# Two recurrences of a hybrid layer on Trainium2: operands of all tokens at once, chunk matrices 64 wide and stacked, inverse beside scan

## What is computed

```
def chunked_gated_delta_rule(q, k, v, g, beta):      # chunks of 64 tokens, gc = cumsum(g) in a chunk
    decay = where(causal, exp(gc_i - gc_j), 0)
    a_mat = where(strict, (k * beta) @ k.T * decay, 0)
    t_inv = inverse(eye + a_mat)
    u = t_inv @ (v * beta);  w = t_inv @ (k * beta * exp(gc))
    attn = q @ k.T * decay
    def step(state, ...):
        v_new = u_n - w_n @ state
        o_n = q_n @ state + attn_n @ v_new
        state = state * exp(gl_n) + k_n.T @ v_new

def rwkv7_scan(r, w, k, v, kk, a):                    # token by token in the reference
    sa = S @ -kk_t
    S = S * w_t + sa * (kk_t * a_t) + v_t * k_t
    o_t = S @ r_t
```

## Time and profile before

| | us |
|---|---|
| median of 3 runs | 3264.71 (3245.12 to 3265.23) |
| the profiled execution's own time | 3262.91 |
| its span | 3260.7 |
| mixer preparation | 338.5 to 386.6 |
| recurrences | 386.8 to 806.1 |

### The profile page before, as it was taken

The page is one execution under the profiler, slowest core; times in us unless marked ns, Lnnn a source line. Parts: engine busy times, 40 slices in busy tenths (PEclk is TensorE's granted clock), DMA queues, the critical chain, the costliest instruction groups (busy, mean ns, idle before and its releaser), DMA issues. The chain is left out here.

```text
span 3260.7 us, 35943 instructions
## 1 busy us (share of the span) xinstructions
PE 2840.7 (87%) x13881; PEld 2265.9 (69%) x13881; DVE 1667.9 (51%) x3102; ACT 1060.9 (33%) x2178; POOL 19.2 (1%) x58
## 2 busy tenths in 40 slices
PE   6967287886899659979899899997997989989999
PEld 5865277775688547657677688885765767768887
DVE  4225555554766355675433566644567543344444
ACT  2215211111432245454422322224454452232221
POOL 0000100000000000000000000000000000000000
PEclk8987578776999879989999999998998999999999
DMA  3210000001666202101133355521210213322221
GB/s 131 92 17 8 14 1 1 1 1 28 201 195 197 85 27 78 52 1 60 49 84 99 116 170 192 187 84 52 78 52 1 82 27 84 99 78 104 103 78 52
DMA packets 212210, 249.42 MB, mean 76 GB/s; under 512 B 13295, under 2 KB 125898, under 8 KB 212042
## 3 DMA queue, kind: packets, MB, share of 16 engines
q1 hardware_dynamic: 177056, 193.30, 18.6%
q10 hardware_dynamic: 34986, 53.84, 5.0%
HBM read 243.70 MB, written 2.10 MB: 75 GB/s over the span
## 5 line engine op out<-in xcount | busy, mean ns | idle before, releaser
L1892 ACT ACTIVATE weights_hi<-weight_ring 128x512 fp32r<-128x512 f32 (+1 forms) x240 | 143.9, 602 | 433.9 <-PE bank L1933 408.5
L1909 DVE TENSOR_TENSOR weights_lo<-weight_ring,weights_hi 128x512 fp32r<-128x512 f32 (+1 forms) x240 | 156.4, 654 | 236.3 <-ACT weights_hi L1892 236.2
L1933 PE MATMUL bank<-h_hi,weights_hi 128*128 128x512 f32 x512 | 209.7, 410 | 16.6 <-DVE h_lo L1909 9.5
L2659 ACT ACTIVATE weights_hi<-weight_ring 128x1024 fp32r<-128x1024 f32 x128 | 135.3, 1057 | 265.5 <-PE bank L2739 264.7
L2739 PE MATMUL bank<-h_hi,weights_hi 128*128 128x512 f32 x512 | 204.3, 399 | 19.4 <-DVE h_lo L340 19.4
L2218 PE MATMUL bank<-chunk_hi,h_hi 128*128 128x512 f32 x448 | 184.7, 412 | 30.4 <-DVE h_lo L340 26.0
L2739 PE MATMUL bank<-h_lo,weights_hi 128*128 128x512 f32 x512 | 204.3, 399 | 0.0
L1933 PE MATMUL bank<-h_lo,weights_hi 128*128 128x512 f32 x512 | 204.1, 399 | 0.0
L1933 PE MATMUL bank<-h_hi,weights_lo 128*128 128x512 f32 x512 | 202.1, 395 | 0.0
L2739 PE MATMUL bank<-h_hi,weights_lo 128*128 128x512 f32 x512 | 201.8, 394 | 0.0
L2739 PE MATMUL bank<-hidden_hi,weights_hi 128*128 128x512 f32 x512 | 200.2, 391 | 0.0
(11 more groups left out here) (446 smaller groups left out, 5757.0 us busy)
## 6 DMA issues: line engine op xcount, KB each, us to landing
arena<-in_ada_w ACTq DMA_DIRECT2D x48, 1024.0 KB, 5.3
weight_ring<-in_w_in SPq DMA_DIRECT2D x21, 2048.0 KB, 7.8
weight_ring<-in_w_in SPq DMA_DIRECT2D x65, 512.0 KB, 5.3
weight_ring<-in_w_mlp_up SPq DMA_DIRECT2D x16, 2048.0 KB, 8.3
weight_ring<-in_w_mlp_down SPq DMA_DIRECT2D x16, 2048.0 KB, 8.1
weight_ring<-in_w_out SPq DMA_DIRECT2D x6, 2048.0 KB, 8.0
weight_ring<-in_w_in SPq DMA_DIRECT2D x10, 1024.0 KB, 6.6
weight_ring<-in_w_branch_a SPq DMA_DIRECT2D x16, 512.0 KB, 6.4
```

The costliest lines, as they stand in the source:

```text
L1892: act.activation(hi, src, ACT.Copy).then_inc(*hi_done.one())
L1909: dve.tensor_tensor(lo, src, hi.bitcast(F32), ALU.subtract).then_inc(*lo_done.one())
L1933: ins = pe.matmul(out, ws[a_][:, n % PIECES, k - k0, :], tile["x"][b_][:, k, :], start=k + a_ + b_ == 0, stop=last[n] and k == k1 - 1 and ...
L2659: act.activation(ws[0][:, t % 2], src[t // 4][:, :, c % 4 * P:c % 4 * P + P], ACT.Copy)\
```

## The change

It rewrites the recurrences in four respects.

1. `mixer_preparation`: `wa` moves into the weight ring. POOL makes more masks: `same`, and for `until`, `strict`, identity and the six levels a packed copy of 64 columns, in which rows 0 to 63 hold the block of chunk 0 and rows 64 to 127 that of chunk 1. DVE waits for the step "masks", and this step now comes right after POOL has zeroed two paddings, in front of all masks.
2. A new stage `operands` forms the operands of all 512 tokens at once, in tensors of 1024 columns (four tiles of 256), gdn first and then rwkv. PE turns and sums, ACT evacuates, takes exponentials and squares, DVE multiplies. The by-feature operands have a pair of heads above each other in the 128 rows.
3. `inverse(kind)`: the chunk matrices are 64 x 64, chunk 0's in rows 0 to 63 and chunk 1's in rows 64 to 127, four heads side by side: 256 columns instead of 512. A product is eight matmuls of 64 x 64 with 64 columns instead of four of 128 x 128 with 128. Each kind has two banks for it.
4. `scan(kind)` has two other banks. `side_by_side` runs five rounds: round i holds the inverses of tile i and the scans of tile i - 1, four generators in turn on each engine. Normalisation, gate and transposes of y are done for each tile within its round.

The diff, cut to its core:

```diff
-        self.bank = [nc.alloc_psum_tensor(f"bank{b}", [P, 512], F32) for b in range(8)]
+        self.banks = nc.alloc_psum_tensor("bank", [P, 8, 512], F32)
+        self.bank = [self.banks[:, b, :] for b in range(8)]
...
                 seq(pool.memset(rwT[:, :, 0:1], 0.0))
+                pool.memset(self.scratch[0:1, 1:2], 0.0).then_inc(*self.pool_ready.step("masks"))
...
-                for m, sign, base in ((self.until, 1, 0), (self.beyond, -1, -1), (self.strict, 1, -1)):
+                for m, sign, base in ((self.until, 1, 0), (self.beyond, -1, -1), (self.strict, 1, -1),
+                                      (self.same, 0, 0)):
...
+                for c in range(2):
+                    rows = slice(c * CH, (c + 1) * CH)
+                    for dst, full in ((self.until_p, self.until), (self.strict_p, self.strict),
+                                      (self.ident_p, self.ident)):
+                        pool.tensor_copy(dst[rows, :], full[rows, rows]).then_inc(*self.pool_order.one())
+                    pool.tensor_copy(self.levels_p[rows], levels[rows, :, rows]).then_inc(*self.pool_order.one())
+                pool.memset(self.scratch[0:1, 0:1], 0.0).then_inc(*self.pool_ready.step("zeros"))
...
-                dve.wait_ge(*self.pool_ready.after("zeros"))
+                dve.wait_ge(*self.pool_ready.after("masks"))
...
+    def operands(self):
...
+                def turn_in(srcT, first, c0, b0):
+                    for i in range(NT):
+                        for c in range(2):
+                            ins = pe.transpose(two(b0)[:, i * MIX + c * P:i * MIX + (c + 1) * P],
+                                               srcT[:, c0 + c, first + i * P:first + (i + 1) * P], self.ident[:])
...
+                did(tt(per_head(tm["kn"]), per_head(two(2)), over(ss[:, 1, :]), ALU.mult), "kn")
+                after("kn")
+                did(tt(per_head(tm["kb"]), per_head(tm["kn"]), over(beta), ALU.mult), "kb")
...
+    def inverse(self, kind, buffers, bank0):
...
+        order = [(s, c) for s in range(H) for c in range(2)]
...
+            def product(out, lhsT, rhs, other=None):
+                for s, c in order:
+                    o = out if other is None or c == 0 else other
+                    ins = pe.matmul(o[rows(c), s * CH:(s + 1) * CH], lhsT(s, c), rhs(s, c), start=True, stop=True)
...
+                product(bank[x], of(M), of(T1)).then_inc(*pe_done.step((i, "X", l)))
+                yield
+                pe.wait_ge(*act_done.after((i, "X", l)))
+                if l > 1:
+                    pe.wait_ge(*dve_done.after((i, "TT", l - 1)))
+                if l < LEVELS - 1:
+                    product(bank[d], of(TT), of(X)).then_inc(*pe_done.step((i, "dT", l)))
+                product(bank[x], of(X), of(TT)).then_inc(*pe_done.step((i, "dTT", l)))
+                yield
...
+    def scan(self, kind, buffers, bank0):
...
+                pe.matmul(last[rows(c), 4 * CH:], self.zeros[rows(1 - c), :],
+                          self.levels_p[rows(1 - c)].rearrange("p l u -> p (l u)")[:, 0:4 * CH], start=True, stop=False)
+                of_state(1 - c, i, c).then_inc(*pe_done.step((i, "RS", c)))
+                yield
+                pe.wait_ge(*pe_done.after((i, "RS", c)))
...
+            yield
+            yield
+            pe.wait_ge(*dve_done.after((i, "y")))
+            for c in range(2):
+                ins = pe.transpose(self.bank[bank0][:, c * P:(c + 1) * P], y[:, c * P:(c + 1) * P], self.ident[:])
...
         def side_by_side(which, engine):
-            running = [p[which](engine) for p in programs]
-            while running:
-                running = [g for g in running if next(g, "end") != "end"]
+            for i in range(NT + 1):
+                running = [p[which](engine, i) for p in inverses if i < NT]
+                running += [p[which](engine, i - 1) for p in scans if i]
+                while running:
+                    running = [g for g in running if next(g, "end") != "end"]
```

More of the change, by code:

```diff
@@ L43 @@
 STOP = None
+KINDS = ("gdn", "rwkv")
 LN_AND_EXP = "natural_log_exp_and_others"
@@ L1223, in _ @@
                 seq(pool.memset(rwT[:, :, 0:1], 0.0))
[L1224 to L1227, removed]
+                pool.memset(self.scratch[0:1, 1:2], 0.0).then_inc(*self.pool_ready.step("masks"))
+                pool.memset(self.zeros, 0.0).then_inc(*self.pool_order.one())
+                pool.memset(levels, 0.0).then_inc(*self.pool_order.one())
+                for m in (self.until, self.beyond, self.strict, self.same):
+                    pool.memset(m, 1.0).then_inc(*self.pool_order.one())
                 seq(pool.memset(self.chunk_of, 1.0))
@@ L1335, in mixer_preparation @@
         self.end_stage("prep")
-    def recurrence(self, kind, take, bank, square):
-        a = self.a
-        gdn = kind == "gdn"
[L1351 to L1393, removed]
@@ L1394, in recurrence @@
         for i in range(NT):
[L1395 to L1396 removed]
+            pe_steps += [(i, "grams"), (i, "T0")] + ([] if gdn else [(i, "GV")])
+            dve_steps += [(i, "LT"), (i, "M", 0), (i, "TT", 0), (i, "masked"), (i, "M", 1)]
+            act_steps += [(i, "T1")]
             for l in range(1, LEVELS):
[L1398 removed]
@@ L1613, in scalar @@
-                for _ in range(5):
-                    yield
-                act.wait_ge(*pe_done.after((i, "O", 1)))
-                act.activation(y[:, i, :], bank[3][:, 0:MIX], ACT.Copy).then_inc(*act_done.step((i, "y")))
-                yield
-            act.wait_ge(*dve_done.after("ss"))
-            seq(act.activation(post, post, ACT.Ln))
-            act.activation(post, post, ACT.Exp, scale=-0.5).then_inc(*act_done.step("rs"))
-            for c in range(2):
-                act.wait_ge(*pe_done.after(("out", c)))
-                act.activation(self.ysT[:, (0 if gdn else 4) + c, :], bank[c][:], ACT.Copy)\
-                   .then_inc(*act_done.step(("out", c)))
@@ new lines, in scalar @@
+                act.wait_ge(*pe_done.after((i, "O", c)))
+                act.activation(y[rows(c), :], last[rows(c), 4 * CH:], ACT.Copy).then_inc(*act_done.step((i, "y", c)))
+            yield
+            act.wait_ge(*dve_done.after((i, "ss")))
+            seq(act.activation(post, post, ACT.Ln))
+            act.activation(post, post, ACT.Exp, scale=-0.5).then_inc(*act_done.step((i, "rs")))
+            yield
+            act.wait_ge(*pe_done.after((i, "out")))
+            act.activation(self.ysT[:, first_y:first_y + 2, i * P:(i + 1) * P],
+                           self.bank[bank0][:, 0:2 * P].rearrange("p (c t) -> p c t", c=2), ACT.Copy)\
+               .then_inc(*act_done.step((i, "out")))
@@ new lines, in scan @@
+        pe_steps, dve_steps, act_steps = [], [("S", 0)], []
+        for i in range(NT):
+            for c in range(2):
+                pe_steps += [(i, "WS", c), (i, "S", c), (i, "RS", c), (i, "O", c)]
+                dve_steps += [(i, "Un", c), (i, "Sd", c), ("S", 2 * i + c + 1)]
+                act_steps += [(i, "y", c)]
+            dve_steps += [(i, "ss"), (i, "y")]
+            act_steps += [(i, "rs"), (i, "out")]
+            pe_steps += [(i, "out")]
+        pe_done.order_of(pe_steps)
```

866 lines of the change are left out of this document (507 added, 359 removed).

## The result

| | before | after |
|---|---|---|
| median of 4 runs, us | 3264.1 (3245.1 to 3265.2) | 3025.4 (3022.4 to 3029.4) |
| ratio | | 0.928, 95% interval 0.925 to 0.931 |
| the profiled execution | 3262.9 | 3029.4 |
| preparation ends | 386.6 | 374.6 |
| operands and recurrences | 419.3 | 44.3 (operands) + 152.0 (five rounds) |

I forecast 3118 with a range of 3030 to 3190.

What follows compares the result with a forecast made beforehand. PE or DVE sets each serial step of a tile's recurrence. 3262.9 - 419.3 + 48 (operands) + 235.5 (rounds: 37 + 3 x 58 + 24.5) + 0.3 (block boundary) - 9 (preparation) = 3118 us; range 3030 to 3190.

Steps and rivals of the forecast that it cites:

- Clock: In all five rounds, half the array works at a time, so TensorE gets 1.2 GHz, granted clock 0.50.
- rival B: In the rounds, pairs count as a full array, so the clock is high: 153 for 235.5 us, 3036 total; chance 0.15.
- Pairs: In inverse and scan, 64-wide matmuls of the two chunks run two at once, 0.213 us a pair at low clock.
- Rivals A and C: Rounds: matmuls follow one another, 3259 us, chance 0.13; each matmul also pays a switch, 3498 us, chance 0.05.
- The wait at the transposes of y: In rounds with inverse and scan, PE waits at y's transposes for rwkv's normalisation on DVE, losing 4 to 5 us.
- Side by side: Scan waits for DVE lie under the inverse's products and the reverse; a round of both takes 58 us.
- Operands: New stage for all tokens: 38 us of DVE work, kn starting after 14 to 21 us; 48 us taken from 47 to 55.
- Preparation: DVE no longer waits for all POOL masks: 9 of 11.9 us saved, bounds 3 and 11.9, allowing for overlap losses.

Runs made afterwards that it cites:

- `patterns_2`: Separate kernel computing nothing of the layer: seven more patterns of 200 fp32 matmuls, behind a pause or 128x128 matmuls; 64x128 with 128 data columns took 0.429 or 0.225 us each.
- `patterns`: Separate kernel computing nothing of the layer: ten patterns of 200 fp32 matmuls, behind a pause or 128x128 matmuls; opposite quadrants behind 128x128 took 0.059 us a matmul.
- `norm_spread`: Changed kernel with y's transposes behind the last level, states zeroed early and normalisation cut into pieces between levels: 3015.4 us, ratio 0.923 to the kernel before.

## Why the forecast was wrong

- **Clock: the step that failed.** "Half of the array works at a time, as at 606 us, so I take 1.2 GHz in all rounds" took two low stretches for a property of the width. The kernel before had both at either level: the Gram products took 5.59 us in tile 1 and 10.57 in tile 2, and three of the four scans began at 1.00. The Gram products at 606 began at the low level and kept it, as 64x128 with 128 columns of data does in `patterns_2`; the scans lost theirs by changes of form, but for the fourth, where the reason is open. The new rounds have their products in opposite quadrants in turn, which lifted the clock in `patterns` and keep it in round 0. At the price of the low clock PE's work was 4 x 35 + 4 x 17 = 208 of the 235.5 us; it was busy for 119.2. Rounds of 37 + 3 x 58 + 24.5 = 235.5 became 22.6 + 41.3 + 35.8 + 36.4 + 15.9 = 152.0; rival B had 153, and 2.8 to 3 us a level for 3.03. Its reason, pairs that count as a full array, is not borne out: 128x128 with 64 columns of data stayed at 0.50 behind a pause. No run has the new rounds at the low clock, so that they would then take 235.5 is not shown. The Trainium skill, "TensorE: Matmul & The Clock Gate", section "The HAM clock gate (the "warmup" mystery)", by which a busy PE gets the full clock, gave the better number for these rounds; but `patterns` has PE busy without a gap for 43 us at 0.50, so busy alone is not the rule.
- **Pairs: right.** Two matmuls of opposite quadrants cost as one, 0.055 us a record at the low clock and 0.030 at the high one. The rule that I set against it (the Trainium skill, "TensorEngine Tiling (Array Packing)", "Gotcha 1: PSUM Pressure") does not show here: one bank or two, 11.88 us. Rivals A and C fell.
- **The wait at the transposes of y: right in place, the size in part by luck.** It is 4.45 us in round 1 and 4.1 in round 2 for 4 to 5, but I had it from a schedule of the low clock (PE free 36 us into the round, DVE done at 42), and PE stood at the transposes after 26. It also cost the clock for about 7 us around and behind it, which I had no term for. At the low clock that I assumed this could not happen.
- **Side by side: little hidden, but not for my reason.** My terms hide 10.5 us (4 x 61.5 = 246 for 235.5), because PE was to be busy nearly all the time; the profiles show 3 (155.0 for 152.0). But PE is busy for 119 of the 152 us, so there was room. Waits for DVE and the low clock behind them took back what the overlap hid, and `norm_spread` hides 7 us a round.
- **Operands: 44.3 for 48,** set by the chain of DVE as I had it (34.6 us busy for 38), with kn at 387.4, 12.6 us after the begin, where I had 14 to 21. PE was not "nearly unbroken" there: busy 25.6 us, idle from 396 to 412, at a mean clock of 0.77. That cost nothing, since DVE set the pace, and PE's last work of the stage brought the clock back to 1.00 at about 416, 3 us ahead of round 0.
- **Preparation: 12.0 for 9.** DVE lost nothing to POOL; POOL lost its pace.

With these in place the sum is 3262.9 - 419.3 + 44.3 + 152.0 - 12.0 = 3027.9 for 3029.4 in the profile.

## What to carry to other kernels

A granted clock in a trace is a state with a history: before taking it as the price of a form, look for the same instructions elsewhere at the other level, and for what pulled them down. Small matmuls are cheap when neighbours in the queue lie in different quadrants of the array (column halves, row halves and opposite quadrants cost the same 0.059 us here) and none changes the form; of these, column halves alone did not lift the clock. Where two chains are put side by side, work that one engine's queue makes wait (a normalisation in one piece) should be cut so that it fits into that engine's gaps.

## What the runs showed that I had not expected

- The clock has a middle ground: one quadrant, column halves, opposite quadrants in blocks of eight, 64x128 with 128 columns of data and 128x128 with 64 keep either level for as long as they ran (12 us and more).
- A matmul of 128 columns of weights costs the same with 64 and with 128 columns of data (0.224 us at 1.00 for 128x128 with 64; the products before took 0.9 for four of 128).
- A change between 64 and 128 rows costs about 0.19 us at the low clock (0.404 us a matmul in turn, for 0.215 of one quadrant) and about 0.14 at the high one (0.211 for 0.118, with two changes in three matmuls).
- POOL's selects take twice as long beside DVE's two-input operations (0.71 us for 0.34), and DVE does not slow down (14 operations in 10.6 us with and without them).
